# A hybrid backbone layer: shift and scale in eight pieces of 256 features, summed with silu(c) standing; the first pair takes its chunks piece by piece

## The chip, the cores and the metric

The kernel runs on one core of one Trainium2 chip. The metric is the device time of one execution in microseconds (us). The kernel before takes 1834.75 us (median of three runs, 1834.39 to 1834.88). A kernel on one core has five engines: TensorE (PE, matrix products), VectorE (DVE), ScalarE (ACT), GpSimd (POOL, idle here) and SyncE (SP, which issues nearly all DMAs).

## The reference

One layer: an HGRN2 mixer and a SwiGLU FFN over 256 latent tokens that follow 256 context tokens, width 2048. Everything is float32. What matters here is how the mixer's input is made:

```
s_lat = silu(c)[:, None, :];  s_ctx = silu(c_ctx)
m_lat = split(s_lat @ w_ada[i] + b_ada[i], 6, axis=-1)        # w_ada is (2048, 6 * 2048)
m_ctx = split(s_ctx @ w_ada[i] + b_ada[i], 6, axis=-1)
a_lat = rms_norm(h_lat, norm_mix) * (1 + m_lat[1]) + m_lat[0]
a_ctx = rms_norm(h_ctx, norm_mix) * (1 + m_ctx[1]) + m_ctx[0]
q, v, g = split(a @ w_in);   z[w] = a @ w_f[w]                # w: two directions; then gated scans per head
```

So each of the 2048 features of `a` needs its own shift (a column of `w_ada`, columns 0 to 2047) and scale (columns 2048 to 4095), and each of those is a sum over all 2048 rows of `w_ada`: 33.6 MB of weights for the four vectors. The products with `w_in` and `w_f` are sums over all features of `a`.

## The kernel before

The order of the work on every engine is written out by hand; engines wait for each other by semaphores, and each engine runs its own list in order. Float32 products are made from two rounded parts: a weight tile `raw` is copied to `whi` by ACT (`hi`, L484), DVE takes the rest into `wlo` (`lo`, L807), and PE makes three products (activation hi by weight hi, lo by hi, hi by lo).

**The modulation stage.** Shift and scale are summed in four quarters `q` of 1024 columns (`ada_column`), each of 16 blocks of 128 rows by 1024 columns (512 KB, rows of 4 KB). PE keeps silu(c) and silu(c_ctx) as four standing columns and streams the weights past them in pieces of 512 columns, two banks for a quarter (`abank`). 40 of the 64 blocks are split (`mod_sum`, L1245 and L1247: four matmuls); 24 are taken whole as float32 (`ada_direct`, L1237: two matmuls, each in two records of the trace). Their slots are three in `work` and three in `arena` (`dslot`). After a quarter ACT copies the four summed rows out (`mod_rows`, L502), PE turns them (`turn_rows`, eight transposes, L1257) and DVE adds the bias and makes shift and scale (`modulation`, L827 to L837).

**x.** Before block 6 of this stage PE turns the norm and bias vectors (L1282, L1283) and x and ctx (`turn_x`, L1275, 64 transposes in 16 groups), DVE evacuates each group (L852), ACT sums squares (L508), PE sums them over features (L1291), ACT copies the result to `rstd` (L542) and DVE multiplies (L874). `modulate` (ACT, L525 twice and L528) applies shift and scale to 128 features of all 512 tokens and makes `ahi`; DVE makes `alo` (`a_lo`, L842).

**The pairs.** Eight pairs of heads follow. A pair takes 16 chunks of 512 KB (256 features of `a` by 256 columns of two weights, rows of 1 KB, two DMAs of 256 KB, L355 and L356): eight chunks VQ (value into banks 0 and 1, query into bank 2; L1296 to L1298 and L1311 to L1313, 36 matmuls of 256 columns) and then eight chunks Z (both directions' gates into banks 0 to 3, 24 matmuls of 512 columns). Beside them run the scans of earlier heads, and from chunk `C_B + 9` on DVE sums the other columns of `w_ada` for the gates and the FFN (`ada`, L903). After the pairs come the output gate, the output projection and the FFN.

## Time and profile before

| | |
|---|---|
| median of three runs | 1834.75 us |
| the profiled execution: its time | 1833.23 us |
| its span (first to last instruction) | 1831.4 us |
| PE busy | 1781.0 us, 97% |
| DVE busy | 1264.1 us, 69% |
| ACT busy | 899.5 us, 49% |
| DMA | 353.82 MB, 193 GB/s in the mean |

All times of the trace are counted from the start of the span. A matmul's record is longer than its share of the engine, since matmuls overlap: what one costs is the distance between starts, which the chain of waits shows.

### The profile page before, as it was taken

Reading aid. Unit: us, or ns where it says so; the run is one execution under the profiler, and the core shown is the slowest. Engines: PE = TensorE matmul, PEld = TensorE weight load, DVE = VectorE, ACT = ScalarE, POOL = GpSimd, SP = SyncE. Lnnn points to the kernel's source line nnn. Section 1 sums busy time; section 2 is a strip of 40 time slices with the busy share of each in tenths; the row PEclk is TensorE's granted clock in tenths of the full one; section 3 lists DMA queues with packets and bytes.
Section 4 is the critical chain, followed back from the end, with each engine's and each line's share of the span. In section 5 each row is a group of like instructions: output and inputs, shape, how many; then the busy total and the mean of one; then the engine's idle time right before and its main releaser. Section 6 shows DMA issues by size and latency. Waiting matters only on the chain.

```text
span 1831.4 us, 25084 instructions
## 1 busy us (share of the span) xinstructions
PE 1781.0 (97%) x9791; PEld 1501.4 (82%) x9791; DVE 1264.1 (69%) x1977; ACT 899.5 (49%) x1279; POOL 0.2 (0%) x4
## 2 busy tenths in 40 slices
PE   8999999999999999999889989999999999999997
PEld 2268989898989898988789878888888888788886
DVE  6753879796979797979985575555555555455755
ACT  6663535454545454545445554444444444455544
POOL 0000000000000000000000000000000000000000
PEclk9999999999999999999999999999999999999999
DMA  9964544554444554444657556777767777655553
GB/s 365 373 231 155 182 145 142 159 158 146 139 150 142 157 173 139 150 139 139 208 183 262 177 160 207 240 227 228 232 212 227 232 227 218 195 195 192 194 192 137
DMA packets 178136, 353.82 MB, mean 193 GB/s; under 512 B 16929, under 2 KB 82786, under 8 KB 176994
## 3 DMA queue, kind: packets, MB, share of 16 engines
q1 hardware_dynamic: 177826, 352.18, 59.8%
q8 instruction: 77, 1.26, 0.3%
q14 instruction: 41, 0.34, 0.1%
q10 hardware_dynamic: 192, 0.05, 0.0%
HBM read 350.06 MB, written 2.11 MB: 192 GB/s over the span
## 4 chain that ended last, share of the span: by engine, by line
PE 85%; DVE 10%; issue 2%; ACT 2%; DMA 1%; ACTq 0%; DVEq 0%
PE bank L1420 9%; PE bank L1422 9%; PE bank L1421 9%; PE bank L1296 8%; PE bank L1298 8%; PE bank L1297 8%; PE bank L1311 3%; PE bank L1312 3%; PE bank L1313 3%; PE bank L1440 3%; PE bank L1442 3%; PE bank L1441 3%; PE score L1500 2%; DVE wlo L807 2%; DVE aacc L903 2%
## 5 line engine op out<-in xcount | busy, mean ns | idle before, releaser
L807 DVE TENSOR_TENSOR wlo<-raw,whi 128x1024 fp32r<-128x1024 f32 x496 | 605.2, 1223 | 439.2 <-ACT whi L484 438.4
L484 ACT ACTIVATE whi<-raw 128x1024 fp32r<-128x1024 f32 x496 | 523.1, 1058 | 668.2 <-PE bank L1422 228.4
L1296 PE MATMUL bank<-ahi,whi 128*128 128x256 f32 (+1 forms) x1024 | 353.5, 345 | 10.6 <-DVE wlo L807 10.3
L1297 PE MATMUL bank<-alo,whi 128*128 128x256 f32 (+1 forms) x1024 | 346.0, 338 | 0.0
L1298 PE MATMUL bank<-ahi,wlo 128*128 128x256 f32 (+1 forms) x1024 | 346.0, 338 | 0.0
L1420 PE MATMUL bank<-whi,ahi 128*128 128x512 f32 x704 | 275.9, 392 | 1.8 <-DVE alo L1138 1.8
L1422 PE MATMUL bank<-whi,alo 128*128 128x512 f32 x704 | 274.7, 390 | 0.0
L1421 PE MATMUL bank<-wlo,ahi 128*128 128x512 f32 x704 | 274.5, 390 | 0.0
L1296 PEld LDWEIGHTS bank<-ahi,whi 128*128 128x128 f32 x1024 | 195.9, 191 | 31.9 <-DVE wlo L807 10.0
L1298 PEld LDWEIGHTS bank<-ahi,wlo 128*128 128x128 f32 x1024 | 196.0, 191 | 20.3
L1297 PEld LDWEIGHTS bank<-alo,whi 128*128 128x128 f32 x1024 | 196.2, 192 | 19.0
L1420 PEld LDWEIGHTS bank<-whi,ahi 128*128 128x128 f32 x704 | 132.4, 188 | 29.3 <-issue 2.2
L1422 PEld LDWEIGHTS bank<-whi,alo 128*128 128x128 f32 x704 | 132.5, 188 | 27.9
L1421 PEld LDWEIGHTS bank<-wlo,ahi 128*128 128x128 f32 x704 | 132.6, 188 | 27.2
L903 DVE SCALAR_TENSOR_TENSOR aacc<-raw,cs,aacc 128x1024 f32<-128x1024 f32 x120 | 153.4, 1279 | 0.5
L1311 PE MATMUL bank<-whi,ahi 128*128 128x256 f32 x512 | 147.3, 288 | 1.3 <-DVE arena L916 1.2
L1313 PE MATMUL bank<-whi,alo 128*128 128x256 f32 x512 | 144.8, 283 | 0.0
L1312 PE MATMUL bank<-wlo,ahi 128*128 128x256 f32 x512 | 144.8, 283 | 0.0
L1311 PEld LDWEIGHTS bank<-whi,ahi 128*128 128x128 f32 x512 | 98.1, 192 | 2.6 <-DVE wlo L807 2.3
L1440 PE MATMUL bank<-whi,ahi 128*128 128x512 f32 x240 | 94.7, 395 | 3.8 <-DVE wlo L807 3.8
L1312 PEld LDWEIGHTS bank<-wlo,ahi 128*128 128x128 f32 x512 | 98.1, 192 | 0.2
L1313 PEld LDWEIGHTS bank<-whi,alo 128*128 128x128 f32 x512 | 98.0, 191 | 0.0
(226 smaller groups left out, 2279.0 us busy)
## 6 DMA issues: line engine op xcount, KB each, us to landing
raw<-in_w_ada_dram SPq DMA_DIRECT2D x168, 512.0 KB, 4.2
raw<-in_ffn_w_gate_dram SPq DMA_DIRECT2D x88, 512.0 KB, 4.4
raw<-in_ffn_w_up_dram SPq DMA_DIRECT2D x88, 512.0 KB, 4.4
raw<-in_ffn_w_down_dram SPq DMA_DIRECT2D x88, 512.0 KB, 4.5
raw<-in_hg_w_in_dram SPq DMA_DIRECT2D x128, 256.0 KB, 3.4
raw<-in_hg_w_f_dram SPq DMA_DIRECT2D x128, 256.0 KB, 3.5
raw<-in_hg_w_in_dram SPq DMA_DIRECT2D x32, 512.0 KB, 4.6
raw<-in_hg_w_o_dram SPq DMA_DIRECT2D x32, 512.0 KB, 4.5
```

Source lines behind the costliest of these rows:

```text
L484: act.activation(whi[:, ck % SPL, :], raw[:, q % RAW, :], ACT.Copy).then_inc(s_hi, 1)
L807: dve.tensor_tensor(wlo[:, ck % SPL, :], raw[:, SEQ["w", ck] % RAW, :], whi[:, ck % SPL, :].bitcast(F32), ALU.subtract).then_inc(s_lo, 1)
L903: dve.scalar_tensor_tensor(out=aacc[:, :], in0=block, scalar=cs[:, k, 0:1], in1=aacc[:, :], op0=ALU.mult, op1=ALU.add).then_inc(s_ac, 1)
L1296: pe.matmul(dst, w, ah, start=start, stop=False, skip_group_check=True)
L1297: pe.matmul(dst, w, al, start=False, stop=False, skip_group_check=True)
L1298: return pe.matmul(dst, wl, ah, start=False, stop=stop, skip_group_check=True)
L1311: pe.matmul(dst, ahi[:, k, tk], whi[:, s, o], start=st, stop=False, skip_group_check=True)
L1312: pe.matmul(dst, ahi[:, k, tk], wlo[:, s, o], start=False, stop=False, skip_group_check=True)
L1313: last = pe.matmul(dst, alo[:, k, tk], whi[:, s, o], start=False, stop=end, skip_group_check=True)
L1420: pe.matmul(dst, ahi[:, k, tk], whi[:, s, o], start=first, stop=False)
L1421: pe.matmul(dst, ahi[:, k, tk], wlo[:, s, o], start=False, stop=False)
L1422: last = pe.matmul(dst, alo[:, k, tk], whi[:, s, o], start=False, stop=end)
```

## The change

It touches the start of the program up to the end of the first pair.

1. Shift and scale come in eight pieces `e` of 256 features. A piece needs eight blocks `n` of 256 rows by 256 columns of shift and 256 of scale: again 512 KB, now as two DMAs of rows of 1 KB. Twelve of the 64 blocks are direct (0, 1, 2, 3, 5 and every eighth from 3 on), 52 are split. Six slots hold them (`dslot`), three further ones the rounded part (`mhi`); the rest `dlow` is written over the raw block. One bank holds a piece's sums: `ob` for the first, `mx` for all others.
2. SP issues x and ctx first (four DMAs of 1 MB), then the bias vector, then the first blocks. PE turns the vectors and x before it sums any block.
3. The first pair takes its chunks alternately: VQ of features 0 to 255, Z of the same features, VQ of the next 256 and so on, as the pieces come. So all seven sums stand in seven banks at once (Z in `score`, `ob` and bank 3). Blocks 0 to 11 come ahead of the first chunk, and four further blocks within each of the first 13 chunks.
4. `modulate` and `a_lo` go by pieces; the constants `keep` and `masks` load at chunk 14, and DVE's sums for the other columns begin at chunk 14 instead of 9 and are as many by chunk 32.

```diff
-    return (2 * (1 - q % 2) + q // 2) * CW
-
-
-X_AT = 6
...
+FIRST = 12
+C_B = 0
+
+
+def mod_direct(n):
+
+    return n in (0, 1, 2, 3, 5) or n % 8 == 3
+
+
+SPLIT_MOD = [n for n in range(64) if not mod_direct(n)]
+
+
+def mod_blocks(ck):
+
+    return list(range(FIRST + 4 * ck, min(FIRST + 4 * ck + 4, 64)))
+
+
...
-            kind = "Z" if p % 16 >= 8 else "VQ"
             tasks = [(j, 4 * g + off) for j, off in tasks_at(p) if 4 * g + off >= 0]
-            yield C_B + g * BODY + p, kind, 2 * g + p // 16, p % 8, tasks
+            if g == 0 and p < 16:
+                yield C_B + p, ("VQ", "Z")[p % 2], 0, p // 2, tasks
+            else:
+                yield C_B + g * BODY + p, "Z" if p % 16 >= 8 else "VQ", 2 * g + p // 16, p % 8, tasks
     for p in range(32):
         yield C_G + p, "G", p // 8, p % 8, tasks_tail(p)
...
+            def load_mod(n):
+
+                if n >= MRAW:
+                    sp.wait_ge(s_du, n - MRAW + 1)
+                e, j = divmod(n, 8)
+                for m in range(2):
+                    sp.dma_start(dslot[n % MRAW][:, m * 512:(m + 1) * 512].rearrange("p (k n) -> p k n", k=2),
+                                 wmod[:, 2 * j:2 * j + 2, m * D + e * 256:m * D + (e + 1) * 256]).then_inc(s_dir[n % MRAW], 16)
+
+            for t in range(4):
+                sp.dma_start(xin[:, t, :], crows[t] if t < 2 else xrows[t - 2]).then_inc(s_x[t], 16)
+            sp.dma_start(brow[0:96, :], b_ada[0].rearrange("(k p) -> k p", p=P)).then_inc(s_vrow, 16)
+            sp.dma_start(vrow[R_ONORM:R_ONORM + 1, :], o_norm).then_inc(s_vrow, 16)
+            for n in range(8):
+                load_mod(n)
...
+                if ck == 1:
+                    for n in range(8, FIRST):
+                        load_mod(n)
+                elif ck >= 2:
+                    for n in mod_blocks(ck - 2):
+                        load_mod(n)
                 load(ck)
-                if ck == C_B + 4:
+                if ck == C_B + 14:
                     sp.dma_start(keep[:, :], keep_in).then_inc(s_keep, 16)
                     sp.dma_start(masks[:, :], masks_in).then_inc(s_keep, 16)
...
+            def mod_hi(n):
+                if mod_direct(n):
+                    return
+                j = SPLIT_MOD.index(n)
+                act.wait_ge(s_dir[n % MRAW], 32 * (n // MRAW + 1))
+                if j >= MHI:
+                    act.wait_ge(s_du, SPLIT_MOD[j - MHI] + 1)
+                if j == MHI - 1:
+                    act.wait_ge(s_ms, 1)
+                act.activation(mhi[j % MHI][:, :], dslot[n % MRAW], ACT.Copy).then_inc(s_mh, 1)
...
+            def mod_rows(e):
+                act.wait_ge(s_du, 8 * (e + 1))
+                if e:
+                    act.wait_ge(s_at, e)
+                act.activation(arow, mod_bank(e)[0:4, :], ACT.Copy).then_inc(s_ar, 1)
...
+            x_rstd()
+            act.wait_ge(s_lb, 1)
+            act.activation(lbt[:, 1, :], lbt[:, 0, :], ACT.Exp).then_inc(s_lb, 1)
+            act.wait_ge(s_ms, 1)
+            act.activation(rstd[:, :], bank[2][:, :], ACT.Copy).then_inc(s_rs, 1)
+            for n in range(4, 8):
+                mod_hi(n)
+            mod_rows(0)
+            mod_hi(8)
+            modulate(0)
+            modulate(1)
+            hi(0)
+            for n in range(9, FIRST):
+                mod_hi(n)
...
-                if ck > C_B + KD // 2:
...
+                if u == 0 and kind == "VQ":
+                    for n in mod_blocks(ck):
+                        mod_hi(n)
+                if u == 0 and kind == "Z" and r < 7:
+                    for n in mod_blocks(ck)[:3]:
+                        mod_hi(n)
+                    modulate(2 * r + 2)
+                    modulate(2 * r + 3)
+                    for n in mod_blocks(ck)[3:]:
+                        mod_hi(n)
+                hi(ck + 1)
+                if u == 0 and kind == "VQ" and r < 7:
+                    mod_rows(r + 1)
+                if kind == "Z" and r == (0 if u else 7):
                     values(u)
...
+            def mod_lo(n):
...
+                dve.wait_ge(s_mh, j + 1)
+                dve.tensor_tensor(dlow[n % MRAW][:, :], dslot[n % MRAW], mhi[j % MHI][:, :].bitcast(F32),
+                                  ALU.subtract).then_inc(s_ml, 1)
...
+            def modulation(e):
...
+                dve.wait_ge(s_at, e + 1)
...
+                dve.tensor_tensor(v, turned[:, :, :, :, 0], each_b, ALU.add).then_inc(s_md, 1)
+                dve.wait_ge(s_md, 3 * e + 1)
+                dve.tensor_tensor(v, turned[:, :, :, :, 1], v, ALU.add).then_inc(s_md, 1)
+                dve.wait_ge(s_md, 3 * e + 2)
+                dve.scalar_tensor_tensor(out=scl[:, 2 * e:2 * e + 2, :], in0=modx[:, 2 * e:2 * e + 2, 1, :], scalar=1.0,
+                                         in1=each_nm, op0=ALU.add, op1=ALU.mult).then_inc(s_md, 1)
...
+            for k in range(4):
+                x_norm(k)
+            dve.wait_ge(s_lb, 3)
+            dve.tensor_tensor(lbt[:, 0, :], lbt[:, 1, :], lbt[:, 2, :], ALU.mult).then_inc(s_lb, 1)
+            for n in range(4, 9):
+                mod_lo(n)
+            modulation(0)
+            x_norm(4)
+            x_norm(5)
+            dve.wait_ge(s_lb, 4)
+            dve.tensor_tensor(lbv, lbt[:, 0, :], lbt[:, 0, :], ALU.subtract).then_inc(s_lb, 1)
+            a_lo(0)
+            a_lo(1)
+            lo(0)
+            for n in range(9, FIRST):
+                mod_lo(n)
...
+                if u == 0 and kind == "VQ":
+                    for n in mod_blocks(ck):
+                        mod_lo(n)
+                    if r < 5:
+                        x_norm(6 + 2 * r)
+                        x_norm(7 + 2 * r)
+                if u == 0 and kind == "Z" and r < 7:
+                    for n in mod_blocks(ck)[:3]:
+                        mod_lo(n)
+                    modulation(r + 1)
+                    a_lo(2 * r + 2)
+                    a_lo(2 * r + 3)
+                    for n in mod_blocks(ck)[3:]:
+                        mod_lo(n)
+                lo(ck + 1)
...
+            if j == 0 and e >= 2:
+                pe.wait_ge(s_md, 3 * e - 1)
+            w = dslot[n % MRAW].rearrange("p (s k n) -> p s k n", s=2, k=2)
+            if mod_direct(n):
+                pe.wait_ge(s_dir[n % MRAW], 32 * (n // MRAW + 1))
+            else:
...
+                pe.wait_ge(s_ml, i + 1)
...
+            for k in range(2):
+                first, end = j == 0 and k == 0, j == 7 and k == 1
+                if mod_direct(n):
+                    last = pe.matmul(mod_bank(e)[0:4, :], csd[:, 2 * j + k, :, :].rearrange("p i s -> p (i s)"),
+                                     w[:, :, k, :], start=first, stop=end, skip_group_check=True)
+                else:
+                    cc = cs4[:, 2 * j + k, :, :].rearrange("p i s -> p (i s)")
+                    pe.matmul(mod_bank(e)[0:4, :], cc, wh[:, :, k, :], start=first, stop=False, skip_group_check=True)
+                    last = pe.matmul(mod_bank(e)[0:4, :], cc, wl[:, :, k, :], start=False, stop=end, skip_group_check=True)
+            last.then_inc(s_du, 1)
...
+            pe.wait_ge(s_vrow, 16 * 6)
+            pe.transpose(score[:, 1, 0:VROWS], vrow[0:VROWS, :], ident[0:VROWS, 0:VROWS])
+            pe.transpose(score[:, 1, 128:224], brow[0:96, :], ident[0:96, 0:96]).then_inc(s_vecT, 1)
...
+            for i in range(KD):
+                turn_x(i)
+            for n in range(FIRST):
+                mod_block(pe, n)
+                if n == 8:
+                    turn_rows(pe, 0)
+                if n == 3:
                     pe.wait_ge(s_one, 1)
                     pe.wait_ge(s_rs, 6)
                     pe.wait_ge(s_xe, KD)
                     pe.matmul(bank[2][:, :], ones[:, :], zt[:, 0, 0, :], start=True, stop=True).then_inc(s_ms, 1)
...
+                    if u == 0 and i < 2:
+                        for n in mod_blocks(ck)[2 * i:2 * i + 2]:
+                            mod_block(pe, n)
+                    if u == 0 and i == 4 and r < 7:
+                        turn_rows(pe, r + 1)
                 last.then_inc(s_used, 1)
...
+                    if u == 0 and i >= 3:
+                        for n in mod_blocks(ck)[i - 3:i - 2]:
+                            mod_block(pe, n)
```

What PE does just ahead of its first chunk, before the change: the last blocks of the fourth quarter, then the first chunk (`bank3` and `ob` are the quarter's banks, `cs4` and `csd` the standing columns, `whi` and `wlo` the split block, `arena` a direct one).

```order
L1245 MATMUL ob<-whi,cs4 4x512
L1247 MATMUL ob<-wlo,cs4 4x512
L1237 MATMUL bank3<-arena,csd 4x512
L1237 MATMUL ob<-arena,csd 4x512
L1245 MATMUL bank3<-whi,cs4 4x512
L1247 MATMUL bank3<-wlo,cs4 4x512
...
L1311 MATMUL bank0<-whi,ahi 128x256
L1312 MATMUL bank0<-wlo,ahi 128x256
```

The same place after the change: block 8, the transposes of piece 0, block 9 (blocks 10 and 11 are cut), then the first chunk's first products and block 12.

```order
L1290 MATMUL mx<-mhi0_55,cs4 4x512
L1291 MATMUL mx<-dlow2_51,cs4 4x512
...
L1299 MATMUL ob<-ident,work 128x4 x4
L1290 MATMUL mx<-mhi1_56,cs4 4x512
L1291 MATMUL mx<-dlow3_52,cs4 4x512
...
L1286 MATMUL mx<-arena,csd 4x512 x2
L1353 MATMUL bank0<-whi,ahi 128x256
L1354 MATMUL bank0<-wlo,ahi 128x256
...
L1290 MATMUL mx<-mhi0_55,cs4 4x512
L1291 MATMUL mx<-dlow0_49,cs4 4x512
```

The transposes of a piece now stand between its own blocks and the first chunk, where before three quarters had been turned long ago.

ACT at the same place after the change, from the copy of `rstd` on (`mhi` is the rounded part of a block, `work<-ob` the summed rows, L559 and L562 are `modulate`):

```order
L568 ACTIVATE rstd<-bank2 128x512
L529 ACTIVATE mhi0_55<-arena 128x1024
...
L535 ACTIVATE work<-ob 4x512
L529 ACTIVATE mhi0_55<-work 128x1024
L559 ACTIVATE arena<-arena,modx,scl 128x256 x2
L562 ACTIVATE ahi<-arena 128x512
...
L506 ACTIVATE whi<-raw 128x1024
L529 ACTIVATE mhi1_56<-arena 128x1024
```

Before the change ACT had the rounded part of a block every row or two, with `modulate` between them:

```order
L542 ACTIVATE rstd<-bank 128x512
L484 ACTIVATE whi<-raw 128x1024
...
L502 ACTIVATE aacc<-ob 4x512
L484 ACTIVATE whi<-raw 128x1024 x4
L525 ACTIVATE arena<-arena,modc,scl 128x256
```

Blocks 9 to 11 now stand behind the summed rows of piece 0, both `modulate` of it and the first chunk's `whi`. And DVE after the change, from its last copy of x on (L880 is `x_norm`, L855 `mod_lo`, L868 to L872 `modulation`, L877 `a_lo`, L839 `lo`):

```order
L894 RECIPROCAL lbt<-lbt 128x16
L880 TENSOR_TENSOR arena<-work,rstd 128x512 x4
L900 TENSOR_TENSOR lbt<-lbt 128x16
L855 TENSOR_TENSOR dlow4_53<-arena,mhi0_55 128x1024
...
L868 TENSOR_TENSOR modx<-ob,bias 128x2x2x2
...
L877 TENSOR_TENSOR alo<-arena,ahi 128x512 x2
L839 TENSOR_TENSOR wlo<-raw,whi 128x1024
L855 TENSOR_TENSOR dlow3_52<-arena,mhi1_56 128x1024
```

The four `x_norm` stand ahead of the first split block, and the piece's shift and scale ahead of block 9.

## Rows read from the trace of the kernel before

**Rows 1.** The page, costliest groups: busy us, mean ns, idle before.

```profile
L807 DVE TENSOR_TENSOR wlo<-raw,whi 128x1024 fp32r<-128x1024 f32 x496 | 605.2, 1223 | 439.2 <-ACT whi L484 438.4
```

**Rows 2.** Busy time by stages: PE, PEld, DVE, ACT, POOL; granted clock, DMA, GB/s.

```profile
26.08:110.65 84.57, 79.42 (x259) 17.80 (x259) 62.81 (x85) 54.24 (x70) 0.00 (x0) 1.00 0.98 362
110.65:146.26 35.61, 35.57 (x297) 35.21 (x296) 16.86 (x21) 24.81 (x38) 0.00 (x0) 1.00 0.51 159
146.26:189.81 43.55, 43.55 (x195) 36.05 (x193) 17.48 (x17) 11.02 (x11) 0.00 (x0) 1.00 0.52 166
```

**Rows 3.** Waits up to 110 us: us in total, times, longest.

```profile
PE score L1245 <- DVE wlo L807: 5.2, 5, 2.9
...
PE bank L1245 <- DVE wlo L807: 2.8, 5, 1.3
```

**Rows 4.** The chain that ended last, 0 to 220 us: start, us, what.

```profile
14.71 1.81 PE score L1237 x4
...
16.85 0.23 PE score L1247
...
18.17 9.66 DVE work L852 x16
...
48.24 0.60 PE mx L1257 x8
49.65 0.60 DVE arena L874
```

**Rows 5.** Timeline of PE: where the stages of the start meet.

```profile
110.65 0.28 PE L1311 MATMUL bank<-whi,ahi 128*128 128x256 f32 x1
...
189.81 0.28 PE L1311 MATMUL bank<-whi,ahi 128*128 128x256 f32 x1
```

**Rows 6.** Busy time in the first 16 us, as Rows 2.

```profile
0.00:4.00 4.00, 0.00 (x0) 0.00 (x0) 0.21 (x3) 0.47 (x1) 0.20 (x4) 1.00 0.45 107
4.00:8.00 4.00, 0.28 (x1) 0.18 (x1) 1.59 (x3) 2.25 (x5) 0.00 (x0) 1.00 1.00 365
8.00:12.00 4.00, 3.84 (x7) 0.72 (x8) 2.16 (x3) 2.12 (x2) 0.00 (x0) 1.00 1.05 417
12.00:16.00 4.00, 4.00 (x14) 0.86 (x12) 1.53 (x2) 3.34 (x3) 0.00 (x0) 1.00 1.00 424
```

**Rows 7.** Timeline of ACT: the third square of x and ctx.

```profile
19.97 1.91 ACT L508 ACTIVATE alo<-arena 128x2048 fp32r<-128x2048 f32 x1 [0.47 <-DMA arena<-in_x_dram]
```

**Rows 8.** Timeline of all engines: vectors turned, mean squares, rstd.

```profile
17.39 0.22 PE L1282 MATMUL mx<-ident,arena 65*128 65x65 f32 x1
...
31.08 1.02 PE L1291 MATMUL bank<-zt,ones 128*128 128x512 f32 x2
...
32.14 0.60 ACT L542 ACTIVATE rstd<-bank 128x512 f32<-128x512 f32 x1 [2.22 <-PE bank L1291]
```

**Rows 9.** Timeline: summed rows copied; one modulate of ACT, then whi.

```profile
41.78 1.06 ACT L502 ACTIVATE aacc<-score 4x512 f32<-4x512 f32 x2 [0.43 <-PE score L1247]
...
73.61 0.59 ACT L525 ACTIVATE arena<-arena,modc,scl 128x256 f32<-128x256 f32 x1
...
75.25 1.04 ACT L484 ACTIVATE whi<-raw 128x1024 fp32r<-128x1024 f32 x1
```

**Rows 10.** Busy time around the first fall of the granted clock, as Rows 2.

```profile
893.00:894.00 1.00, 0.00 (x0) 0.00 (x0) 1.00 (x2) 0.98 (x2) 0.00 (x0) 1.00 0.54 209
...
896.00:897.00 1.00, 1.00 (x7) 1.00 (x6) 1.00 (x2) 0.00 (x0) 0.00 (x0) 0.50 0.95 270
...
899.00:900.00 1.00, 1.00 (x9) 1.00 (x8) 1.00 (x5) 0.42 (x1) 0.00 (x0) 0.84 0.83 317
```

**Rows 11.** Busy time where rows of 1 KB are loaded, as Rows 2.

```profile
156.00:158.00 2.00, 2.00 (x10) 1.65 (x9) 0.00 (x0) 0.57 (x1) 0.00 (x0) 1.00 0.91 312
...
134.00:136.00 2.00, 2.00 (x19) 2.00 (x18) 1.29 (x2) 0.62 (x1) 0.00 (x0) 1.00 0.90 273
```

**Rows 12.** Timeline of DVE in the second pair: the low part of chunk 24.

```profile
220.10 1.22 DVE L807 TENSOR_TENSOR wlo<-raw,whi 128x1024 fp32r<-128x1024 f32 x1
```

More of the change, by code:

```diff
@@ L175, in build @@
                  + [arena[:, 4 * D + 2 * P + i * CW:4 * D + 2 * P + (i + 1) * CW] for i in range(3)])
+        dlow = ([over(f"dlow{i}", "work", KD * TT + i * CW, [P, CW]) for i in range(3)]
+                + [over(f"dlow{i + 3}", "arena", 4 * D + 2 * P + i * CW, [P, CW]) for i in range(3)])
+        mhi = [over("mhi0", "zt", 2 * TT, [P, CW]), over("mhi1", "aacc", 0, [P, CW]), over("mhi2", "zt", 0, [P, CW])]
         ident = sb("ident", [P, P])
@@ L519, in modulate @@
             def modulate(k):
[L521 removed]
+                act.wait_ge(s_md, 3 * (k // 2 + 1))
                 act.wait_ge(s_xn, k + 1)
@@ L673, in _ @@
                     gate_sigmoid((ck - C_B) // 16 - 1, p - 2)
-                if kind == "Z" and r == 0:
+                if kind == "Z" and r == (0 if u else 7):
                     queries(u)
@@ L879, in _, with x_norm @@
-            lo(C_B)
-            lo(C_B + 1)
-            modulation(3)
-            for k in range(8, KD):
-                a_lo(k)
-                if k % 2 == 1:
-                    lo(C_B + k // 2 - 2)
-            for i in range(6, KD // 2 + 2):
-                lo(C_B + i)
+            def x_norm(k):
+                dve.tensor_tensor(xn[:, k, :], xT[:, k, :], rstd[:, :], ALU.mult).then_inc(s_xn, 1)
+            dve.wait_ge(s_vecT, 1)
+            dve.tensor_copy(vec[:, :], score[:, 1, 0:VROWS]).then_inc(s_vec, 1)
@@ L1072, in _ @@
                     clip_gates((ck - C_B) // 16 - 1)
-                if kind == "Z" and r == 1:
+                if ck == C_B + 16:
+                    scale_queries(0)
+                if kind == "Z" and r == 1 and u:
                     scale_queries(u)
@@ L1254, in turn_rows @@
+            last.then_inc(s_du, 1)
+        def turn_rows(pe, e):
+            pe.wait_ge(s_ar, e + 1)
+            if e == 0:
                 pe.wait_ge(s_vec, 2)
-            for f in range(8):
-                o = 32 * (2 * (q % 2) + q // 2) + 4 * f
-                last = pe.transpose(mx[:, o:o + 4], arow[:, f * P:(f + 1) * P], ident[0:4, 0:4])
+            for f in range(4):
+                last = pe.transpose(mod_bank(e)[:, 4 * f:4 * f + 4], arow[:, f * P:(f + 1) * P], ident[0:4, 0:4])
@@ L1303, in v_bank @@
                 first, end = k == 0, k == KD - 1
-                if first and u:
+                if first and u == 1:
+                    pe.wait_ge(s_vev, half + 1)
+                elif first and u:
                     pe.wait_ge(s_zc, 4 * (u - 1) + 1 + 2 * half)
@@ L1318, in q_bank @@
                 first, end = k == 0, k == KD - 1
-                if first and u:
+                if first and u == 1:
+                    pe.wait_ge(s_qev, 1)
+                elif first and u:
                     pe.wait_ge(s_zc, 4 * (u - 1) + 2)
@@ L1334, in z_bank @@
                             pe.wait_ge(s_av, ada_ended(ck))
-                if first and f < 2:
+                if first and f < 2 and u:
                     pe.wait_ge(s_vev, 2 * u + f + 1)
-                if first and f == 2:
+                if first and f == 2 and u:
                     pe.wait_ge(s_qev, u + 1)
                 o = slice(512 * a + f * P, 512 * a + (f + 1) * P)
-                return three(bank[f][:, :], whi[:, s, o], wlo[:, s, o], ahi[:, k, :], alo[:, k, :], first, end)
+                return three(z_out(u, f), whi[:, s, o], wlo[:, s, o], ahi[:, k, :], alo[:, k, :], first, end)
             def beside(ck, between):
@@ L1597, in ada_chunk @@
         return C_FF + 12 + 80 * (e - 6) + 5 * k
-    begin = ADA_ENDS[e - 1] + 1 if e else KD // 2 + 1
+    begin = ADA_ENDS[e - 1] + 1 if e else 14
     return C_B + begin + k * (ADA_ENDS[e] - 2 - begin) // (KD - 1)
```

242 lines of the change are left out of this document (66 added, 176 removed).

## The prediction

> **What bounds the kernel now.** I read the table of stages first. Up to 110.65 us the kernel sums shift and scale: DMA share 0.98 and 362 GB/s, but PE is busy for 79.42 of the 84.57 us from 26.08 on [rows 2], and in all of the stage it waits for DVE's low parts for only 8.0 us (5.2 + 2.8) [rows 3]. DMA looks like the bound and PE is one too. The first pair follows: VQ until 146.26, Z until 189.81 [rows 2, 5], PE busy throughout, DMA at half of its share (0.51, 0.52) and DVE at under half. So the merge puts an almost full PE stage and a full PE stage together. What it can win on PE is only the 8 us of waits and what the blocks get cheaper; what it can lose is every gap in which PE has nothing to do because shift and scale of the first piece aren't there.
>
> **Prices.** From the chain of waits [rows 4]: a direct block (two matmuls, four records) 1.81 us, and 0.10 at the change back to split products (I take 1.91); a split block four times 0.23, so 0.93; a copy of a group of x 9.66 / 16 = 0.60; one product of x and rstd 0.60; eight transposes of summed rows 0.60, so four are 0.30 and with 0.10 on each side 0.5. A VQ chunk: 35.61 us [rows 2] less 0.8 for the fourth quarter's transposes, by 8, is 4.35. A Z chunk: 43.55 / 8 = 5.44. ACT's rounded part is 1.05 [rows 9], DVE's low part 1.22 [rows 1] (1.15 back to back).
>
> **The new start.** (1) The bias vector stands behind 4.26 MB (identity 0.07, x and ctx 4.19) on SP's queue, and PE turns the vectors before x. The first 12 us carried 0.43 + 1.46 + 1.67 = 3.56 MB, the next ones 424 GB/s [rows 6], so 4.26 MB are through at 13.7. The third square of ACT waited for x until 19.97 [rows 7]; ahead of it stood 6.45 MB (six blocks, identity, vectors, three of x), through by the same count at 18.8. So a transfer is seen 1.2 us after its bytes: 14.9. (2) Before, the vectors' transposes began at 17.39 and the copies of x at 18.17 [rows 8, 4]; with 0.2 for the load ahead and 0.2 for a lower-bound step that now stands between, the copies begin at 16.1 and end at 25.8; PE is free 1.75 earlier, as it was before (26.08 against 27.83), at 24.1. (3) Blocks 0 to 3 are direct: 4 x 1.81, 31.3. The mean square and ACT's copy take 31.08 to 32.74 in the trace, 1.66 [rows 8]: rstd at 33.0. (4) DVE now makes four products with rstd (2.4) and a small step (0.2) ahead of the low part of block 4 (1.25): 36.9. PE has waited 4.7 us. Blocks 4 to 7: 0.93 + 1.91 + 2 x 0.93, 41.6. (5) Summed rows 0.8 (half of 1.06 [rows 9] and the signals), block 8 by ACT 1.05 and DVE 1.25, PE 0.93, transposes 0.5: 46.2; PE has waited 3.1. (6) Three small DVE steps 0.8, two modulate of 1.64 each (73.61 to 75.25 [rows 9]), ACT's part of the first chunk 1.05 and of block 9 1.05, then DVE's low part of the chunk is done and that of block 9 ends at 53.7: PE has waited 7.5. Blocks 9, 10 and 11: 0.93, 0.2 for DVE, 0.93, 1.91. The first chunk starts at 57.8.
>
> (7) The clock. At 893 us PE had nothing to do in the trace, and the granted clock stood at 0.50, 1.2 instead of 2.4 GHz, from 896 until into 899 [rows 10]: some 3.3 us, in which half is lost, 1.7. The new start has gaps of 4.7 and 7.5 us, longer than the longest wait for DVE up to 110 us, 2.9 [rows 3]. I take two such falls, 3.4 us, bounds 0 (no fall) and 7 (each of the three gaps and the start). First chunk: 61.2. The Trainium skill says the same under "TensorE: Matmul & The Clock Gate", Part 1: the clock is throttled by default and activity releases it. By that rule the gaps cost more here than in a stage that is held up evenly; the trace agrees with its fall at 896.
>
> **From the first chunk on.** PE alone: 8 x (4.35 + 5.44) = 78.3, 46 split blocks 42.8, 6 direct 11.5, seven turns 3.5: 136.1. A round of two chunks and eight blocks is 9.79 + 6.5 + 1.9 + 0.5 = 18.7 us. Beside it DVE has 7 low parts of blocks and 2 of chunks (10.8), four products and low parts of `a` (2.5), 0.8: 14.1. ACT has 9 rounded parts (9.5), two modulate (3.3), rows 0.6: 13.4. DMA moves ten blocks, 5.24 MB, which is 281 GB/s; rows of 1 KB went at 312 GB/s with a share of 0.91 and 273 with 0.90 [rows 11], so 303 to 343 when full. All fit, so PE sets the pace, and the first pair ends at 61.2 + 136.1 = 197.3, against 189.8 [rows 5]: 7.5 us later.
>
> **Check by differences.** PE does 12 direct blocks less and 12 split more: -11.8. It begins real work at 14.9 instead of 8.2: +6.8. It has 15.3 us of gaps instead of 8.0: +7.3. Eight turns of 0.5 instead of four of 0.8: +0.8. Clock +3.4 less what the cold start costs before, at most 2. Sum +4.5 to +6.5. The two counts agree within 3; I take +7.
>
> **Edits at nothing.** DVE's sums for the other columns (`ada`, 1.28 each) start at chunk 14: three more fall behind the first pair, two more before chunk 24. The low part of chunk 24 ends at 221.3 [rows 12], PE wants it at 189.8 + 8 x 4.35 = 224.6; 2.6 us fit in 3.3. If they don't, each us over costs one. Values and queries leave their banks during the last Z chunk (two table loads and three copies, some 5 us in 5.4), the clips no longer hold the second pair's first products, and keep and masks are wanted at chunk 21. After the first pair nothing else moves.
>
> **The sum.** 1833.23 (the profiled execution, span 1831.4) + 7 = 1840; the median of the runs stands 1.5 above the profiled one, so 1842.
>
> **Rivals.** A measurement of this kernel tells 0.2%, 3.7 us, from no change.
> *The rounds don't keep PE's pace* (0.18). All pieces but the first are summed in `mx`, so the first block of piece r + 2 waits until DVE has read piece r + 1, and DVE does that behind the low parts of three blocks. By the prices: block 15 used at 5.3 us of the round, rows at 5.9, three rounded parts until 9.0, the low part of the third until 10.6, DVE's second step at 11.1; PE wants to write at 11.25. So the margin is 0.15 us, and each us that a load, ACT or DVE is late costs PE one, in six rounds. Slower loads do the same: at 260 GB/s a round is 20.2 us instead of 18.7, +9. One to three us a round give +6 to +18 more: 1848 to 1860. What decides is whether block 14 of a round is in before 8 us.
> Only a page says the worst of it: the Trainium skill, "DMA: Bandwidth & Descriptors", Measured, asks for 1 MiB a DMA for 75% of the peak, with about 2 us fixed for each; by it 256 KB alone would run at 101 GB/s and the stage at over 400 us. The rows don't bear it out, because transfers overlap.
> *Within 0.2%* (0.18). The clock doesn't fall in the gaps (-3.4), and DVE's parts come 1 us sooner at two places: 1833 to 1838.
> *Faster* (0.09). The vectors come early. If the bias vector doesn't wait for all of x, the copies of x run as x lands and end 2.4 us after the last quarter, at 17.5 instead of 25.8: 8 us less, the first chunk at 53, and the first pair ends at 189.3; with no fall of the clock too, at 186: 1831 to 1830. From 11 us saved on it is faster. Against it: one queue, in order, and the square of x that waited in turn [rows 7].
>
> **How the numbers follow.** Forecast 0.55 (+4 to +12, 1838 to 1847), the rounds 0.18, no difference 0.18, faster 0.09. Slower than 1838.4 is 0.73, within 0.18, faster 0.09. For eight in ten I leave out the faster case and the far end of the rounds: 1834 to 1855; the forecast alone is 1838 to 1847.
>
> **What would show it.** After: PE's first transpose of x at about 15 us; PE idle at 32 to 37, 42 to 45 and 46 to 54 us, granted clock 0.50 behind them; the first chunk at 58 to 62; from there PE full, 18 to 19 us a round; the second pair at 197. Wrong would be: a first chunk before 54, rounds over 20 us with PE waiting for DVE, or a stall in the second pair.

## The result and the profile after

The changed kernel takes 1842.09 us (median of 6 runs, 1839.08 to 1845.13) against 1834.57 us (6 runs on the same chip). The ratio is 1.0047, 95% interval 1.0036 to 1.0059: slower, by about 0.47%. The forecast was 1842, with 0.73 on slower.

The head of the page of the profiled execution, with PE's share:

```profile
span 1841.4 us, 25227 instructions
...
PE 1774.6 (96%) x9791; PEld 1506.7 (82%) x9791; DVE 1278.5 (69%) x1993; ACT 909.2 (49%) x1291; POOL 0.2 (0%) x4
```

The same view of stages as [rows 2], cut at PE's first turn of a vector, at the first chunk and at the second pair:

```profile
0.00:14.13 14.13, 0.28 (x1) 0.18 (x2) 0.59 (x5) 9.07 (x12) 0.20 (x4) 1.00 0.85 329
14.13:61.84 47.71, 32.92 (x121) 14.09 (x121) 27.78 (x44) 17.87 (x27) 0.00 (x0) 0.82 0.61 196
61.84:199.36 137.52, 137.52 (x718) 90.12 (x717) 91.75 (x110) 89.77 (x114) 0.00 (x0) 1.00 0.84 268
0.00:199.36 199.36, 170.72 (x838) 104.39 (x838) 120.12 (x158) 116.71 (x152) 0.20 (x4) 0.96 0.79 255
199.36:1841.40 1642.04, 1603.92 (x8955) 1402.30 (x8953) 1158.36 (x1837) 792.52 (x1139) 0.00 (x0) 0.99 0.58 185
```

Read it from the bottom. Behind the start of the second pair the kernel takes 1642.04 us; before it was 1831.4 - 189.81 = 1641.6. So in these two traces all of the difference lies ahead of it: 199.36 against 189.81 [rows 5], 9.55 us. From the first chunk on, PE is busy for 137.52 of 137.52 us. What is lost is lost ahead of the first chunk, where PE is idle for 47.71 - 32.92 = 14.79 us, with a mean granted clock of 0.82.

PE's timeline ahead of the first chunk (start, duration, in brackets the idle time before and who ended it):

```profile
14.13 0.37 PE L1309 MATMUL score<-ident,arena 65*128 65x65 f32 x1 [8.24 <-DMA arena<-in_hg_o_norm_dram]
...
14.45 10.14 PE L1320 MATMUL bank<-ident,arena 128*128 128x128 f32 x64
24.52 5.31 PE L1286 MATMUL ob<-work,csd 128*4 128x512 f32 x12
...
37.05 0.59 PE L1290 MATMUL ob<-mhi,cs 128*4 128x512 f32 x1 [4.44 <-DVE dlow L855]
...
38.84 3.58 PE L1286 MATMUL ob<-arena,csd 128*4 128x512 f32 x4
...
47.57 0.39 PE L1290 MATMUL mx<-mhi,cs 128*4 128x512 f32 x1 [2.88 <-DVE dlow L855]
...
56.42 0.59 PE L1290 MATMUL mx<-mhi,cs 128*4 128x512 f32 x1 [7.43 <-DVE dlow L855]
...
61.84 0.38 PE L1353 MATMUL bank<-whi,ahi 128*128 128x256 f32 x1
```

The three gaps are 4.44, 2.88 and 7.43 us. The direct block at 38.84 takes 3.58 us, where twelve records of direct blocks at 24.52 took 5.31. The granted clock (column before the DMA share) says why:

```profile
36.00:38.00 2.00, 0.95 (x3) 0.34 (x4) 2.00 (x2) 0.08 (x1) 0.00 (x0) 0.57 0.54 189
38.00:40.00 2.00, 2.00 (x5) 0.22 (x3) 1.26 (x2) 0.00 (x0) 0.00 (x0) 0.50 0.03 5
...
48.00:50.00 2.00, 0.99 (x7) 0.40 (x5) 0.91 (x4) 0.37 (x1) 0.00 (x0) 0.98 1.04 366
...
52.00:54.00 2.00, 0.00 (x0) 0.00 (x0) 0.80 (x2) 1.97 (x4) 0.00 (x0) 0.50 0.11 38
...
58.00:60.00 2.00, 2.00 (x6) 0.46 (x5) 1.24 (x2) 1.06 (x1) 0.00 (x0) 0.50 0.22 50
60.00:62.00 2.00, 2.00 (x5) 0.35 (x6) 1.52 (x2) 1.06 (x1) 0.00 (x0) 0.96 0.91 303
```

It falls to 0.50 (1.2 instead of 2.4 GHz) twice: at 36.3 us, inside the gap of 4.44, and just before 50 us, 1 us after the gap of 7.43 began and 2.4 us behind the end of the gap of 2.88. It is back at 43.1 and at 60.2 us. The Trainium skill has this as "TensorE: Matmul & The Clock Gate", Part 1, a clock that is throttled by default and released by activity; the trace agrees in the falls and in the return under work, but the column reads 1.00 at the start of the span too, where PE is idle.

The chain across the last gap shows what it is made of:

```profile
49.02 0.18 DVE modx L868
...
49.63 1.10 ACT arena L559 x2
...
51.29 1.09 ACT arena L559 x2
...
52.93 1.05 ACT whi L506
54.00 1.23 DVE wlo L839
55.23 1.15 DVE dlow L855
56.42 0.59 PE mx L1290
```

Only the last step belongs to block 9. The two modulates and the chunk's rounded and low part (49.63 to 55.23) are not what block 9 needs; they merely stand ahead of it on ACT and on DVE. That is a question of order, which the experiments take up.

### The profile page after: what moved, and what is told of

It is laid out like the page before. It is cut to its first block, busy times and chain, and to the rows that moved or that the text cites. A ratio compares the mean times of both kernels' runs of the same rounds, so it can differ in the third digit from the quotient of the medians.

```text
span 1841.4 us, 25227 instructions
## 1 busy us (share of the span) xinstructions
PE 1774.6 (96%) x9791; PEld 1506.7 (82%) x9791; DVE 1278.5 (69%) x1993; ACT 909.2 (49%) x1291; POOL 0.2 (0%) x4
## 3 DMA queue, kind: packets, MB, share of 16 engines
q1 hardware_dynamic: 203426, 352.18, 60.2%
q8 instruction: 77, 1.26, 0.3%
## 4 chain that ended last, share of the span: by engine, by line
PE 87%; DVE 8%; issue 2%; ACT 1%; DMA 1%; SPq 0%; ACTq 0%; DVEq 0%
PE bank L1470 9%; PE bank L1472 9%; PE bank L1471 9%; PE bank L1336 7%; PE bank L1337 7%; PE bank L1338 7%; PE bank L1353 3%; PE bank L1354 3%; PE bank L1355 3%; PE bank L1490 3%; PE bank L1491 3%; PE bank L1492 3%; PE score L1552 2%; PE score L1490 1%; PE score L1491 1%
## 5 line engine op out<-in xcount | busy, mean ns | idle before, releaser
L839 DVE TENSOR_TENSOR wlo<-raw,whi 128x1024 fp32r<-128x1024 f32 x456 | 557.3, 1224 | 383.6 <-ACT whi L506 383.2
L506 ACT ACTIVATE whi<-raw 128x1024 fp32r<-128x1024 f32 x456 | 481.2, 1058 | 602.9 <-PE bank L1472 228.3
L1336 PE MATMUL bank<-ahi,whi 128*128 128x256 f32 (+1 forms) x976 | 333.9, 342 | 11.1 <-DVE wlo L839 10.9
L1337 PE MATMUL bank<-alo,whi 128*128 128x256 f32 (+1 forms) x976 | 326.5, 335 | 0.0
L1338 PE MATMUL bank<-ahi,wlo 128*128 128x256 f32 (+1 forms) x976 | 326.4, 334 | 0.0
L1336 PEld LDWEIGHTS bank<-ahi,whi 128*128 128x128 f32 x976 | 186.0, 191 | 32.1 <-DVE wlo L839 10.8
L1338 PEld LDWEIGHTS bank<-ahi,wlo 128*128 128x128 f32 x976 | 186.0, 191 | 18.5
L1337 PEld LDWEIGHTS bank<-alo,whi 128*128 128x128 f32 x976 | 186.2, 191 | 17.3
```

Of the source, the lines that this page charges most:

```text
L506: act.activation(whi[:, ck % SPL, :], raw[:, q % RAW, :], ACT.Copy).then_inc(s_hi, 1)
L839: dve.tensor_tensor(wlo[:, ck % SPL, :], raw[:, SEQ["w", ck] % RAW, :], whi[:, ck % SPL, :].bitcast(F32), ALU.subtract).then_inc(s_lo, 1)
L1336: pe.matmul(dst, w, ah, start=start, stop=False, skip_group_check=True)
L1337: pe.matmul(dst, w, al, start=False, stop=False, skip_group_check=True)
L1338: return pe.matmul(dst, wl, ah, start=False, stop=stop, skip_group_check=True)
```

## The experiments

Each kernel is the changed one with the edit shown. I read each trace at two places, the first chunk and the start of the second pair, because what follows the second pair differs between single executions: from 1637.1 to 1643.8 us in the traces of the changed kernel and its nine variants, for the same code there. An effect of one or two us is read at the second pair, the ratio checks it. The start scatters too: the change and experiments 4 and 5 have the same code ahead of the first chunk, and reach it at 61.84, 62.20 and 61.12 us. So one trace tells the start to about half a us.

| run | first chunk | second pair | ratio to before | 95% |
|---|---|---|---|---|
| before | | 189.81 | 1 | |
| the change | 61.84 | 199.36 | 1.0047 | 1.0036 to 1.0059 |
| 1 vectors first | 55.84 | 193.37 | 1.0018 | 1.0009 to 1.0027 |
| 2 gaps filled | 46.84 | 184.38 | 0.9974 | 0.9965 to 0.9983 |
| 3 clock kept | 57.83 | 195.42 | 1.0022 | 1.0014 to 1.0031 |
| 4 split in rounds | 62.20 | 196.37 | 1.0036 | 1.0023 to 1.0048 |
| 5 step late | 61.12 | 202.70 | 1.0066 | 1.0054 to 1.0079 |
| 6 = 1 + 2 | 42.37 | 179.97 | 0.9939 | 0.9926 to 0.9951 |
| 7 = 1 + 2 + 4 | 42.95 | 177.10 | 0.9926 | 0.9913 to 0.9940 |
| 8 = 7 + clock | 43.32 | 177.54 | 0.9929 | 0.9917 to 0.9942 |
| 9 = 7 + clock, fitted | 40.70 | 175.55 | 0.9916 | 0.9902 to 0.9929 |

### 1. The vectors ahead of x

```diff
+            sp.dma_start(brow[0:96, :], b_ada[0]...).then_inc(s_vrow, 16)
+            sp.dma_start(vrow[R_ONORM:R_ONORM + 1, :], o_norm).then_inc(s_vrow, 16)
             for t in range(4):
                 sp.dma_start(xin[:, t, :], ...).then_inc(s_x[t], 16)
-            sp.dma_start(brow[0:96, :], b_ada[0]...).then_inc(s_vrow, 16)
-            sp.dma_start(vrow[R_ONORM:R_ONORM + 1, :], o_norm).then_inc(s_vrow, 16)
```

> SyncE issues the bias vector and o_norm ahead of the four quarters of ctx and x instead of behind them; nothing else is changed, PE still turns the vectors before x. Theory (the start is held by the order of one queue, so PE's first transpose of x waits for 4.26 MB): the transposes of x begin when the first quarter lands, 7 to 9 us instead of 14.45, and end 2.4 us after the last one, at 17 to 18 instead of 24.5; the first chunk starts at 54 to 55 instead of 61.9, the second pair at 192 instead of 199.4, and the kernel takes 7 to 8 us less, about 1834.5, which is the time before the change. Rival (the first pair has slack behind the first chunk, or the low parts and the mean square hold the start and not x): the transposes come early but the first chunk stays within 2 us of 61.9, and the time stays at 1841 to 1842.

PE's timeline in this run:

```profile
8.94 0.37 PE L1309 MATMUL score<-ident,arena 65*128 65x65 f32 x1 [5.22 <-DMA arena<-in_hg_lb_logits_dram]
...
9.26 9.84 PE L1320 MATMUL bank<-ident,arena 128*128 128x128 f32 x64
19.03 5.31 PE L1286 MATMUL ob<-work,csd 128*4 128x512 f32 x12
```

The order of one queue did hold the start: the first turn comes at 8.94 instead of 14.13 and the second pair 6.0 us earlier; the ratio falls by 0.29%, 5.3 us. Of the 6.0 us, 5.2 are the earlier turn; 0.8 came later (PE's work on x shorter by 0.3, the clock back 0.5 us sooner) and is no more than the scatter of the start. It is less than the 7 to 8 us that I expected, because from 9.26 on x isn't late any more: PE and DVE need 9.84 us for the sixteen groups (9.6 to 10.4 in the ten traces with this start), so they end at 19.0 and not at 17 to 18. DVE's copies show a part of it that I hadn't priced (DVE's timeline of this run):

```profile
10.36 0.69 DVE L891 COPY work<-bank 128x512 f32<-128x512 f32 x1 [0.25 <-PE bank L1320]
11.21 0.69 DVE L891 COPY work<-bank 128x512 f32<-128x512 f32 x1 [0.16 <-PE bank L1320]
...
12.92 7.86 DVE L891 COPY work<-bank 128x512 f32<-128x512 f32 x13 [0.16 <-PE bank L1320]
```

The first come 0.85 us apart and wait for PE each time; from the fourth on they follow at 7.86 / 13 = 0.60, DVE's own pace.

### 2. The gaps filled

ACT and DVE get the same work in another order. ACT:

```diff
+            mod_hi(4)
+            mod_hi(6)
             act.wait_ge(s_ms, 1)
             act.activation(rstd[:, :], bank[2][:, :], ACT.Copy).then_inc(s_rs, 1)
-            for n in range(4, 8):
-                mod_hi(n)
-            mod_rows(0)
+            mod_hi(7)
+            hi(0)
             mod_hi(8)
+            mod_rows(0)
+            mod_hi(9)
+            mod_hi(10)
             modulate(0)
             modulate(1)
-            hi(0)
-            for n in range(9, FIRST):
-                mod_hi(n)
```

DVE likewise: the low parts of blocks 4 and 6 ahead of the wait for rstd, those of block 7, the chunk and block 8 ahead of the summed rows, those of 9 and 10 behind its small steps on shift and scale and ahead of the two low parts of `a`. Two of the four products with rstd move behind the low part of block 8.

> Same work in another order on ACT and DVE ahead of the first chunk: the rounded and low parts of blocks 4 and 6 come ahead of ACT's wait for the mean square and DVE's first products with rstd, those of the first chunk and of block 8 ahead of the summed rows of the first piece, those of blocks 9 and 10 ahead of the two modulate. Nothing is left out, PE's order is as it was. Theory (PE's three gaps of 4.4, 2.9 and 7.4 us are the order on ACT and DVE, and two of them bring the clock down for 6.8 and 10.2 us): no wait of PE for DVE over 2 us before the last step to the first chunk, granted clock 1.0 but for one short fall, first chunk at 45 to 50 instead of 61.9, the whole 12 to 16 us shorter: 1826 to 1830. Rival (the chain of x, rstd, summed rows, modulate and the low part of a is itself as long as the start, so that filling its gaps moves nothing): the gaps shrink in number but one long wait ahead of the first chunk takes their place, first chunk over 57, time within 4 us of 1842.

```profile
31.56 0.79 PE L1295 MATMUL ob<-mhi,cs 128*4 128x512 f32 x1
...
38.64 0.39 PE L1295 MATMUL mx<-mhi,cs 128*4 128x512 f32 x1 [1.43 <-DVE dlow L856]
...
41.86 0.59 PE L1295 MATMUL mx<-mhi,cs 128*4 128x512 f32 x1 [1.79 <-DVE dlow L856]
...
46.84 0.39 PE L1358 MATMUL bank<-whi,ahi 128*128 128x256 f32 x1
```

The gaps of 4.44, 2.88 and 7.43 us are 0 (and 0.24 ahead of a later block), 1.43 and 1.79 us. The first chunk starts 15.0 us earlier, the second pair too, and the ratio falls by 0.73%, 13.4 us: with this order the change is a gain over the kernel before (0.9974). The rival is out: what the first chunk needs was not the bound of this stretch, the order on ACT and DVE was. In the stretch from the first turn to the first chunk PE's idle time fell from 14.79 to 3.56 us (11.2 us) and its busy time from 32.92 to 29.15 (3.8 us, most of it the clock). The clock was not wholly kept: it is at 0.50 from 41.1 to 44.5 us, and blocks 9 and 10 take 3.17 us there instead of the 2.16 that they take in experiment 3, which costs about 1 us.

### 3. The clock kept

```diff
+                for _ in range({4: 18, 8: 10, 9: 32}.get(n, 0)):
+                    pe.matmul(bank[0][:, 0:P], ones[:, :], ident[:, :], start=True, stop=True)
```

> PE gets useless matmuls of 128 x 128 by 128 columns (ones by the identity, into a bank that is free) in the three gaps: 18 ahead of the wait for block 4, 10 ahead of block 8, 32 ahead of block 9. Nothing is left out. It takes the fall of the clock out and leaves the gaps. Theory (the clock costs by itself: blocks 4 to 7 and 9 to 11 ran at 1.2 GHz, the direct blocks at 3.51 instead of 1.81 us): granted clock 1.0 from 19 us on, blocks 7 and 11 take 1.8, first chunk 3 to 4 us earlier at 58 to 59, time 1838 to 1839. Rival (the half clock is hidden, since the next wait for DVE follows in any case): the gaps grow by what the blocks get faster, first chunk within 1 us of 61.9, time 1841 to 1842.

```profile
32.69 4.18 PE L1327 MATMUL bank<-ident,ones 128*128 128x128 f32 x36
...
38.30 1.88 PE L1286 MATMUL ob<-arena,csd 128*4 128x512 f32 x4
```

The direct block takes 1.88 instead of 3.58 us, the granted clock is 1.00 in every 2 us of this stretch, and the second pair starts 3.94 us earlier; the ratio falls by 0.25%, 4.6 us, and the time of 1836.6 us lies below the 1838 to 1839 that I expected. So the two falls cost 3.9 us by themselves, to about half a us, and PE's idle time proper some 11 more (experiment 2 took the idle time and some three quarters of the clock's part).

### 4. The rounds' direct blocks split

```diff
-    return n in (0, 1, 2, 3, 5) or n % 8 == 3
+    return n in (0, 1, 2, 3, 5, 11)
```

> Six of the ten remaining direct blocks (one in each round) are summed as split products, which are cheaper on PE (0.93 for 1.91 us) and dearer on ACT (1.05) and DVE (1.25). Theory (PE alone sets the pace of the rounds): each round falls from 18.9 to 17.9, the second pair starts 5.9 us earlier at 193.5, time about 1836. Rival (the rounds are held by DVE's step from the summed rows into the bank that is handed on, or by loads of 1 KB rows): a round stays at 18.9 or gets longer because ACT and DVE have one block more, PE waits for DVE or for the blocks' low parts, time 1842 or more.

PE's timeline: the transposes of two pieces' summed rows, 18.35 us apart (18.90 in the changed kernel), and the wait between them.

```profile
69.76 0.41 PE L1299 MATMUL mx<-ident,work 4*128 4x4 f32 x4
...
78.95 0.39 PE L1290 MATMUL mx<-mhi,cs 128*4 128x512 f32 x1 [0.27 <-DVE dlow L855]
...
88.11 0.41 PE L1299 MATMUL mx<-ident,work 4*128 4x4 f32 x4
```

Neither side has it all. From the first chunk to the second pair it is 134.17 instead of 137.52 us, 3.35 less where 5.9 was expected, and the time is 1839.7 where the theory said 1836. PE's busy time there is 132.47, so 5.05 less: a direct block is 5.05 / 6 = 0.84 dearer for PE, not 0.98. And PE waits six times 0.28 us for the low part of the block that was direct, 1.7 in all. PE sets the pace of the rounds, with DVE close behind.

This trace shows something else, ahead of its first chunk, where its code is that of the changed kernel. Block 8 began at 46.84, behind a gap of 2.88 us, and the gap of 7.43 came after the transposes:

```profile
47.54 0.50 PE L1291 MATMUL mx<-dlow,cs 128*4 128x512 f32 x1
47.98 0.59 PE L1299 MATMUL ob<-ident,work 4*128 4x4 f32 x4
```

In the changed kernel these records last 0.40 us each. Here the clock had fallen at 47.7 us, with PE at work and before the long gap began.

### 5. DVE's step late

```diff
+                    if r < 6:
+                        dve.wait_ge(s_xn, 2 * r + 6)
+                        for k in (2 * r + 4, 2 * r + 5):
+                            dve.tensor_tensor(xn[:, k, :], xT[:, k, :], rstd[:, :], ALU.mult)
                     modulation(r + 1)
```

> DVE repeats two products of x and rstd (1.2 us, the same values into the same place) ahead of its step on the summed rows, in six of the seven rounds; the rest is as in the changed kernel. Nothing is left out. It prices the margin of the bank mx that is handed from one piece to the next, which the prediction put at 0.15 us. The changed kernel's trace has DVE's second step end at 91.56 and PE's load for the next block at 91.93, so the margin is at most 0.4 us. Theory (PE sets the pace, DVE is 0.4 us short of it): PE waits some 0.8 to 0.9 us for DVE in each of six rounds, a round takes 19.7 instead of 18.9, the second pair starts 5 us later at 204.5, time about 1847. Rival (margin 0.15): 1.05 a round, 6.3 us. Rival (the rounds have slack beyond this wait, PE is not their pace): less than 1 us in all, 1841 to 1843.

In the changed kernel DVE's second step and PE's next block in `mx` stand so, with the rows transposed at 88.27:

```profile
91.39 0.17 DVE L870 TENSOR_TENSOR modx<-mx,modx 128x8 f32<-128x8 f32 x1
...
92.15 0.40 PE L1290 MATMUL mx<-mhi,cs 128*4 128x512 f32 x1
```

And in this run:

```profile
88.33 0.41 PE L1303 MATMUL mx<-ident,work 4*128 4x4 f32 x4
...
92.67 0.17 DVE L870 TENSOR_TENSOR modx<-mx,modx 128x8 f32<-128x8 f32 x1
...
92.89 0.40 PE L1294 MATMUL mx<-mhi,cs 128*4 128x512 f32 x1 [0.52 <-DVE modx L870]
...
107.89 0.41 PE L1303 MATMUL mx<-ident,work 4*128 4x4 f32 x4
```

DVE's step ends 4.51 us behind the transposes instead of 3.29, 1.22 later, and a round takes 19.56 instead of 18.90, 0.66 more. The margin of the hand-off is therefore 1.22 - 0.66 = 0.56 us, more than the 0.15 of the prediction and than the expectation's 0.4, which I had read up to the start of PE's load; up to the matmul's start, 92.15, it is 0.59. From the first chunk to the second pair it is 141.58 us, 4.06 more (6 x 0.66 = 4.0), less than the 5 that the theory said; the rival with a margin of 0.15, 6.3 us, is out. The mechanism of the rival "the rounds don't keep PE's pace" is real; it did not start in the change because the margin held.

### 6 and 7. Together

> The edits of the first two experiments together: the vectors ahead of x on SyncE's queue, and the order on ACT and DVE that fills the gaps ahead of the first chunk. Theory (two separate costs of the start, 5.5 and 13.8 us, that add up): first chunk at 41 to 42, second pair at 179, time 1822 to 1824. Rival (with the start 5.5 us earlier the loads don't keep up: in the second experiment the DMA share was 1.02 to 1.11 from 34 to 58 us): PE waits for blocks or chunks of weights in the first rounds, first round over 20 us, and the two together win less than 17 us: 1825 to 1828.

> The edits of the sixth run and the six direct blocks of the rounds as split products. Theory: another 3 us as alone (each round 18.35 instead of 18.9, with PE's wait of 0.27 us for a low part in each): 1819 to 1821. Rival (loads or ACT are short by now): no further gain, within 1 us of the sixth run.

Windows of the sixth run, ahead of the first chunk and in the first rounds:

```profile
30.00:32.00 2.00, 1.83 (x8) 0.52 (x8) 2.00 (x4) 1.64 (x2) 0.00 (x0) 1.00 1.06 366
...
42.00:44.00 2.00, 2.00 (x12) 1.12 (x11) 1.95 (x2) 0.84 (x1) 0.00 (x0) 1.00 1.11 350
```

The second pair starts 19.4 us earlier than in the changed kernel, where the two edits alone gave 6.0 and 15.0; the ratio falls by 1.08%, 19.8 us, and the time of 1823.0 is the one that the theory gave. The 1.6 us that are missing from the sum are about the scatter of three single starts; that the edits take something from each other is not shown. The rival foresaw DMA as the next bound. DMA is full here (share 1.06 to 1.11, 350 to 366 GB/s in these windows), yet PE waits for none of it from the first chunk to the second pair: it is busy for 137.60 of 137.60 us. The six split blocks give 2.9 us at the second pair and 2.4 by the ratios (within their intervals), as much as alone.

### 8 and 9. And the clock

The useless products of experiment 3 in the kernel of the seventh run, first 10 and 14 of them, then 6 and 7.

> The seventh run's kernel with useless matmuls (10 ahead of block 8, 14 ahead of block 9) that keep PE at work in the two short gaps that are left; nothing is left out. Theory (after gaps of 1.43 and 1.79 us the clock stood at 0.50 for 3 us in the second experiment, and half of that is lost): 1 to 2 us less than the seventh run, 1818 to 1819, granted clock 1.0 throughout the start. Rival (the step behind the gap, the low part of the first chunk, is what the first chunk waits for anyway): the same as the seventh run within 0.5 us.

> As the eighth run, with 6 and 7 useless products in place of 10 and 14. In that run one product took 0.24 us (20 records in 2.39, 28 in 3.39), so they lasted 2.3 and 3.3 us where the gaps of the seventh run were 1.75 and 1.79, and PE came late by what they were too long. Theory (the clock does cost the start 1.5 us: the seventh run needs 5.53 us from block 9 to the first chunk, 37.42 to 42.95, the eighth 3.85, 39.47 to 43.32): with products that fit the gaps the first chunk starts 1.5 us earlier than in the seventh run, at 41 to 41.6, and the time is 1817 to 1818. Rival (what the first chunk waits for isn't PE): first chunk at 42.5 to 43 as in the seventh run, time 1819 to 1820.

The seventh run behind its last gap, and the ninth:

```profile
37.42 0.40 PE L1295 MATMUL mx<-mhi,cs 128*4 128x512 f32 x1 [1.79 <-DVE dlow L856]
...
40.36 2.66 PE L1291 MATMUL mx<-arena,csd 128*4 128x512 f32 x4
42.95 0.38 PE L1358 MATMUL bank<-whi,ahi 128*128 128x256 f32 x1
```

```profile
36.74 0.39 PE L1295 MATMUL mx<-mhi,cs 128*4 128x512 f32 x1
...
38.90 1.88 PE L1291 MATMUL mx<-arena,csd 128*4 128x512 f32 x4
40.70 0.39 PE L1360 MATMUL bank<-whi,ahi 128*128 128x256 f32 x1
```

The eighth run gained nothing (second pair 0.4 us later than in the seventh), so its theory missed: the clock stayed up, but the products were longer than the gaps. They put block 9 off by 1.3 us. PE was also done with x 1.05 us sooner (18.64 against 19.69), and lost that again in a wait of 1.26 us for the low part of block 7: block 6 comes ahead of it on ACT and DVE, and ACT waited for its load until 27.10. With the products fitted to the gaps, block 9 to the first chunk takes 3.96 instead of 5.53 us, and the second pair starts 1.55 us earlier. In time the ninth run and the seventh can't be told apart (0.9916 and 0.9926, intervals overlap; medians 1819.2 and 1819.1), and the 1817 to 1818 that I expected did not show. The ninth run has the earliest second pair and the lowest ratio of the study: 1819.2 us, 14.5 below the 1833.7 of the kernel before on the same chip.

## Why the prediction was right

The mechanism was the predicted one and so was the place; most sizes held, some only in sum.

**Steps 1 and 2, the new start.** The vectors were there at 14.1 and not at 14.9, and PE's transposes of x began at 14.45. But PE was free at 24.52, not 24.1: "copies at 0.60 each" left out that PE's first groups come 0.85 us apart. The two errors nearly cancel: DVE's copies of x began 0.55 us sooner and took 1.0 longer. Experiment 1 shows that the late vectors cost 5 to 6 us.

**Steps 3 to 6, the gaps.** Blocks 0 to 3 were done at 31.5 (31.3 predicted), rstd at 33.25 (33.0), the low part of block 4 at 37.0 (36.9). The gaps were 4.44, 2.88 and 7.43 us where 4.7, 3.1 and 7.5 stood. Adding ACT's and DVE's queues in program order gave a start that no trace had shown yet to within 0.3 us a gap. Experiment 2 shows that another order wins 15.0 us of the gaps and their clock.

**Step 7, the clock.** 3.4 us predicted, 3.9 measured (experiment 3). The count of two falls came out so. Their place did so only in part: the second fall is not the work of the long gap alone. It came 1 us into it in the changed kernel, and in experiment 4, with the same code there, 0.8 us behind the gap of 2.88 and ahead of the long one. The long gap is where it lasted. First chunk at 61.8 against 61.2.

**From the first chunk on.** PE alone, as predicted, but 137.5 instead of 136.1 us. The mis-sized term is the round: 18.90 for 18.7, seven times. By the distances between starts in the changed kernel's trace, the excess is in the chunks: the eight Z chunks take 45.3 us instead of 43.5 and the eight VQ chunks 35.8 instead of 34.8, the 46 split blocks 43.3 instead of 42.8. The direct blocks (10.9 for 11.5) and the seven turns (2.3 for 3.5) are cheaper than their prices. A chunk whose products stand between blocks is dearer than one by itself: before, the same products took 43.6 and 35.0 us; why is not shown. Experiment 4 agrees on the direct block, 0.84 more than a split one and not 0.98.

**The check by differences** gave +4.5 to +6.5 where +9.55 was measured at the second pair, and the step that failed is "15.3 us of gaps instead of 8.0: +7.3". Of the 8.0 us of waits in [rows 3] the longest, 2.9, ended at 8.16 us, at the start of PE's first block. The term "begins real work at 14.9 instead of 8.2" had it already, so it was taken off twice. By windows PE's idle time rose from 7.9 to 13.9 us ahead of the first work (+6.0) and from 5.3 to 14.8 in the gaps (+9.5), 15.5 in all, while its busy time up to the second pair fell from 176.7 to 170.7 (-6.0). 15.5 - 6.0 = 9.5. With the 2.9 given back the check says +7.4 to +9.4, and the first count, 7.5, lies within it. (Two of the sums are off by 0.1: 14.9 - 8.2 is 6.7, and the first chunk without the clock comes to 57.7.)

**The median** agreed with 1842 partly by luck: +7 was added to the profiled execution, +9.55 is what the profile shows at the second pair, and the medians differ by 7.5 (the ratio's interval is 6.6 to 10.8 us).

**The rivals.** "The rounds don't keep PE's pace" had its mechanism right and its margin too small, 0.56 instead of 0.15 us; its second half, slower loads, did not come: PE never waited for DMA in the rounds, even at 350 GB/s. The rule of the Trainium skill that was set beside it ("DMA: Bandwidth & Descriptors", the 1 MiB from Measured and the fixed 2 us from Anatomy of one DMA, both for DMAs that GpSimd issues) would by that estimate have made the stage three times as long. Here SyncE issues the loads; those in pieces of 256 KB went at 348 to 350 GB/s from 14 to 22 us in the changed kernel, and the trace disagrees with the rule wherever transfers are queued behind one another. "Faster" took 8 us for early vectors and called 11 the point where it decides; the six us that they give leave the kernel at 1.0018, still slower than before. "Within 0.2%" needed the clock not to fall and DVE's parts sooner; without the falls alone the ratio is 1.0022 (1.0014 to 1.0031), at the edge of it.

**Edits at nothing.** No stall in the second pair. That what follows its start takes 1642.04 us against 1641.59 says little, since it differs by up to 6.7 us between executions. But over the second pair's eight VQ chunks PE is busy for 34.79 of 34.79 us in both traces, and for 110.19 of the 110.19 us from the start of the second pair, with the moved `ada` sums in them.

So the merging isn't the loss. Its stage is full on PE, and PE's busy time up to the second pair fell by 6.0 us. By the distances between starts the blocks take 10.9 us less (the falls of the clock in it), the transposes of x 1.5 more, the first pair's chunks 2.4 more and the rest 0.8 more, 6.1 less by this count. The prediction's prices had neither the 1.5 nor the 2.4. What the merge won was spent ahead of the first chunk: 15.0 us on the order of ACT and DVE (11.2 of them idle time of PE, most of the rest the clock) and 5 to 6 on the place of two small transfers. With both put right the same change is a gain of 0.6%.

## What to carry to other kernels

When two stages are merged, work out the stretch ahead of the merged loop by its own queues: what stands in program order ahead of the first operand that PE can use, on each engine and on the DMA queue. An operation that waits for a late value (rstd, summed rows) should stand behind all that needs no such value. Two short vectors behind 4 MB on one queue cost 5 to 6 us here; a gap of PE on this path cost its length and, where the granted clock fell, half of PE's speed in the work that followed, until the clock was back. When gains are checked by differences, give every wait one owner: a wait ahead of the first product belongs either to the start or to the gaps.
